# Sums and turnings of the first projection between later token spans, input rows asked for first, and modulation stores on other queues

## The reference, cut to what matters

```
for l in range(2):
    sh1, s1, g1, sh2, s2, g2 = split(silu(c) @ ada_w[l] + ada_b[l], 6)   # one set for latent, one for context tokens
    a = rmsnorm(h, norm_mix[l]) * (1 + s1) + sh1
    y = mixer_ab(a) if l == 0 else mixer_c(a)      # gated DeltaNet + short conv | windowed attention with sinks
    h = h + g1 * y
    f = rmsnorm(h, norm_ffn[l]) * (1 + s2) + sh2
    h = h + g2 * hier_moe(f)                       # top-2 of 32 experts
return rmsnorm(h_latent, norm_final)

def mixer_ab(a):                                   # its first step is the projection that this case is about
    z = a @ w_in                                   # columns: q, k, v, gate, two rates per head, b, c, h
    q, k, v = split(silu(conv3(z[qkv])), 3)
    q, k = l2norm(q), l2norm(k)                    # sums of squares over the 128 channels of a head
    ...                                            # delta rule over chunks, gated by silu(gate)
    y_short = b * conv3(c * h)
```

## Time and profile before

| | |
|---|---|
| median of 3 runs | 3735.29 us (3731.69 to 3741.27) |
| the profiled execution | 3731.38 us, its span 3729.6 us |
| TensorE busy | 3034.7 us, 81% of the span |
| VectorE, ScalarE, GpSimd busy | 1220.7, 677.5 and 330.9 us |
| mean granted TensorE clock | 0.922 of full speed |
| `project0`, its seven parts (L510) | 1344 matmuls, 496.5 us busy |

### The profile page before, as it was taken

One profiled execution on the slowest core, in us unless ns is written; L12 is line 12 of the kernel. 1 busy time (PEld: TensorE's weight loads), 2 busy tenths in 40 slices (PEclk: granted clock), 3 DMA queues, 4 the chain that ended last, 5 costly groups with the idle time before them and its releaser, 6 DMA issues. The chain is left out here.

```text
span 3729.6 us, 50996 instructions
## 1 busy us (share of the span) xinstructions
PE 3034.7 (81%) x18238; PEld 1579.8 (42%) x18239; DVE 1220.7 (33%) x2215; ACT 677.5 (18%) x1522; POOL 330.9 (9%) x366
## 2 busy tenths in 40 slices
PE   3899999799976957999998729958889579789991
PEld 1454455588862433333333214445554323223330
DVE  3313313467664342111111061246653511001114
ACT  2212112111121110000000031146661100000002
POOL 0000000121210000000000032211110000000002
PEclk9999999899997977999999959979999689999995
DMA  6411110223234436778988351131101379886874
GB/s 268 149 49 51 35 44 28 80 77 97 70 142 172 175 159 262 292 302 337 395 312 325 145 210 39 40 126 52 42 22 47 153 293 398 332 370 252 359 298 163
DMA packets 152814, 667.46 MB, mean 179 GB/s; under 512 B 26128, under 2 KB 62128, under 8 KB 121936
## 3 DMA queue, kind: packets, MB, share of 16 engines
q1 hardware_dynamic: 123568, 540.05, 37.8%
q0 software_dynamic: 19504, 72.03, 5.2%
q10 hardware_dynamic: 9584, 53.19, 3.4%
HBM read 595.84 MB, written 69.39 MB: 178 GB/s over the span
## 5 line engine op out<-in xcount | busy, mean ns | idle before, releaser
L1808 PE MATMUL bank<-w,xT 128*64 x3392 | 752.7, 602 | 67.2 <-DMA w<-in_moe_w 41.1
L510 PE MATMUL bank<-aT,w 128*128 128x512 f32 (+1 forms) x1344 | 496.5, 532 | 6.7 <-DVE short L692 5.9
L1808 PEld LDWEIGHTS bank<-w,xT 128*64 128x64 f32 x3392 | 254.1, 139 | 529.5 <-issue 529.3
L1828 PE MATMUL bank<-w,hT 128*64 (+1 forms) x1696 | 380.3, 601 | 55.3 <-issue 49.0
L510 PEld LDWEIGHTS bank<-aT,w 128*128 128x128 f32 x1344 | 263.6, 197 | 234.8 <-issue 219.8
L1900 DVE TENSOR_TENSOR h<-h,bank 128x512 f32<-128x512 f32 x53 | 36.5, 688 | 787.1 <-PE bank L1808 787.1
L1828 PEld LDWEIGHTS bank<-w,hT 128*64 128x64 f32 x1696 | 121.9, 138 | 277.3 <-issue 277.3
L2108 PE MATMUL bank<-at_w_in,aT 128*128 128x512 f32 x416 | 182.3, 598 | 2.9 <-PEq L116 2.9
L2299 PE MATMUL bank<-eye,probs 128*128 128x128 f32 x640 | 99.0, 286 | 45.2 <-ACT probsT L2363 45.0
L1757 POOL DMA_INDIRECT x<-moe_x,idx_block x55 | 53.3, 970 | 841.4 <-PE bank L1784 839.7
L2108 PEld LDWEIGHTS bank<-at_w_in,aT 128*128 128x128 f32 x416 | 79.1, 192 | 99.8 <-issue 99.8
(11 more groups left out here) (339 smaller groups left out, 3924.7 us busy)
## 6 DMA issues: line engine op xcount, KB each, us to landing
w<-in_moe_w SPq DMA_DIRECT2D x180, 2048.0 KB, 8.9
ada_w<-in_ada_w SPq DMA_DIRECT2D x48, 1024.0 KB, 7.9
moe_y<-y ACTq DMA_DIRECT2D x53, 512.0 KB, 10.4
w<-in_moe_w ACTq DMA_DIRECT2D x12, 2048.0 KB, 31.5
w<-in_ab_w_in SPq DMA_DIRECT2D x28, 512.0 KB, 3.8
moe_y<-zero POOLq DMA_DIRECT2D x1, 8192.0 KB
moe_x<-a SPq DMA_DIRECT2D x13, 512.0 KB, 2.6
at_w_in<-in_at_w_in SPq DMA_DIRECT2D x3, 2048.0 KB
```

Of the source, the lines that this page charges most:

```text
L510: mm = pe.matmul(k.bank[3 * s + n][:, 0:width], w[j][:, c, :], aT[:, c, at:at + width], start=(c == 0), stop=(c == KC - 1))
L1808: mm = pe.matmul(k.bank[UP[half]][u * UNIT:(u + 1) * UNIT, :], xT[:, c, u * UNIT:(u + 1) * UNIT], w13[:, r if u else ds(buf[0], 1), half, ...
L1828: mm = pe.matmul(k.bank[Y[half]][u * UNIT:(u + 1) * UNIT, :], hT[:, c, u * UNIT:(u + 1) * UNIT], w2[:, r if u else ds(buf[0], 1), at:at + ...
```

## The change

1. `begin`: SP asks for the context rows and two halves of the latent rows, each on its own semaphore, ahead of the table pieces; `eye` and `tri` come behind them. Each sum of squares waits only for its own rows. SP stores the modulation rows. POOL has nothing to do.
2. `norm_mod` and `gate_heads`: SP instead of ACT stores the modulation rows. `project_norm`: POOL stores them.
3. `project0`: a part is now made of single spans (`span`), and `turns` of single groups. The sums of k stand after two spans of part 3, the turnings of k in two pieces between the spans of part 4, those of v between the spans of part 5. ACT's square roots become `roots`, put after its next copy; ACT takes part 4 into a new tile `c_raw` before the turnings of v.
4. `combine`, layer 0: ACT takes the sum of squares of tile n-3 right after it scales tile n.
5. `attend`: `v_win` gets a semaphore of its own, which only the output products wait for.

```diff
 begin, SP
+        sp.dma_start(k.H[:, 0:CT, :], dr["ctx"].rearrange("b (t p) d -> p (b t) d", p=P)).then_inc(h_in[0], 16)
+        for n in range(2):
+            half = slice(n * LT // 2, (n + 1) * LT // 2)
+            sp.dma_start(k.H[:, CT + n * LT // 2:CT + (n + 1) * LT // 2, :], x[:, half, :]).then_inc(h_in[1 + n], 16)
         mod.loads(sp)
+        sp.dma_start(k.eye[:], dr["const_eye"]).then_inc(consts_in, 16)
+        sp.dma_start(k.tri[:], dr["const_tri"].rearrange("d p n -> p d n")).then_inc(consts_in, 16)
+        mod.store(sp)
+        sp.wait_ge(consts_in, 32)
 begin, ACT and DVE
-        act.wait_ge(h_in, 64)
         for n, t in enumerate(ours):
+            act.wait_ge(h_in[(t + 2) // 4], 16)
...
-        mod.store(act)
 norm_mod and gate_heads (project_norm likewise, on POOL)
+            mod.store(sp)
...
-            mod.store(act)
 project0, TensorE
+        def span(h, j, n):
+            s, (at, width) = j % 2, SPANS[n]
+            if n == 0:
+                pe.wait_ge(w_in[j], primed((h + 1) * 16))
+                pe.wait_ge(z_copied[s], primed(h * COPIED[s] + use(j)))
+                pe.wait_ge(z_gated[s], primed(h))
+            for c in range(KC):
+                mm = pe.matmul(k.bank[3 * s + n][:, 0:width], w[j][:, c, :], aT[:, c, at:at + width],
+                               start=(c == 0), stop=(c == KC - 1))
+            if n == 2:
+                mm.then_inc(z_ready[s], 1)
...
             part(h, 2)
+            span(h, 3, 0)
+            span(h, 3, 1)
             norms(h, 1)
-            part(h, 3)
-            turns(h, 0)
-            part(h, 4)
-            turns(h, 1)
-            part(h, 5)
+            span(h, 3, 2)
+            span(h, 4, 0)
+            span(h, 4, 1)
+            turns(h, 0, 0)
+            turns(h, 0, 1)
+            span(h, 4, 2)
+            turns(h, 0, 2)
+            span(h, 5, 0)
+            turns(h, 1, 0)
+            turns(h, 1, 1)
+            span(h, 5, 1)
+            turns(h, 1, 2)
+            span(h, 5, 2)
             part(h, 6)
 project0, ACT
             square(h, 0)
+            roots(h, 0)
...
             square(h, 1)
             raw(h, 2, x)
+            roots(h, 1)
...
             silu(h, 2)
+            act.wait_ge(z_gated[1], primed(h))
+            raw(h, 4, c_raw)
             take_turns(h, 1)
-            raw(h, 4, z)
 combine, ACT
+            if not final and n >= 3:
+                square(n - 3)
 attend
-            sp.dma_start(vw[u][:], ...).then_inc(blk_in[u], 16)
+            sp.dma_start(vw[u][:], ...).then_inc(vw_in[u], 16)
...
+            if kv == 0:
+                pe.wait_ge(vw_in[u], primed(g // KVS // 2 * 16 + 16))
```

More of the change, by code:

```diff
@@ L246, in begin @@
     c = k.sb("c", [P, 2, KC])
-    c_in, c_silu, h_in = k.sem("c_in", 0), k.sem("c_silu", 0), k.sem("h_in", 0)
+    c_in, c_silu, h_in = k.sem("c_in", 0), k.sem("c_silu", 0), [k.sem(f"h_in{n}", 0) for n in range(3)]
+    consts_in = k.sem("eye_tri_in", 0)
     mod = Modulation(k, [(0, 0)], KC, 0)
@@ L258, in _ @@
         sp.dma_start(c[:, 1, :], dr["c"].rearrange("a (p j) -> (a p) j", p=P)).then_inc(c_in, 16)
-        mod.loads(sp)
[L261 to L267, removed]
+        sp.dma_start(k.H[:, 0:CT, :], dr["ctx"].rearrange("b (t p) d -> p (b t) d", p=P)).then_inc(h_in[0], 16)
+        x = dr["x"].rearrange("b (t p) d -> p (b t) d", p=P)
+        for n in range(2):
+            half = slice(n * LT // 2, (n + 1) * LT // 2)
+            sp.dma_start(k.H[:, CT + n * LT // 2:CT + (n + 1) * LT // 2, :], x[:, half, :]).then_inc(h_in[1 + n], 16)
+        mod.loads(sp)
+        sp.dma_start(k.eye[:], dr["const_eye"]).then_inc(consts_in, 16)
+        sp.dma_start(k.tri[:], dr["const_tri"].rearrange("d p n -> p d n")).then_inc(consts_in, 16)
+        mod.store(sp)
+        sp.wait_ge(consts_in, 32)
     @block.tensor
@@ L285, in _ @@
         nc.scalar.activation(rstd[:], rstd[:], ACT.Sqrt).then_inc(root_ready, 1)
-        mod.store(act)
     @block.vector
     def _(dve):
-        dve.wait_ge(h_in, 64)
         for n, t in enumerate(theirs):
+            dve.wait_ge(h_in[(t + 2) // 4], 16)
             if n:
@@ L349, in _ @@
                     nc.scalar.copy(aT[:, 4 * half:4 * half + 4, at:at + P], src).then_inc(aT_ready, 1)
-        if mod:
-            mod.store(act)
     @block.vector
@@ L401, in project0 @@
     y = k.sb("y", [P, PADTOK])
+    c_raw = k.sb("c_raw", [P, PADTOK])
     z = k.sb("z", [P, PADTOK])
@@ L501, in _ @@
         pe.wait_ge(ab_read, primed(1))
-        def part(h, j):
[L504 to L512, removed]
+        def span(h, j, n):
[9 more added lines that the diff above has]
+                mm.then_inc(z_ready[s], 1)
+        def part(h, j):
+            for n in range(3):
+                span(h, j, n)
         def aux(h, m):
@@ L526, in norms, with turns @@
                           start=True, stop=True).then_inc(norm_ready, 1)
-        def turns(h, n):
+        def turns(h, n, g):
             if n == 0:
@@ L533, in turns @@
                 pe.wait_ge(silu_ready, primed(h * 3 + 3))
[L534 to L540, removed]
+            to = aux(h, 6 + 3 * n + g)
+            for q in range(min(4, NT - 4 * g)):
+                t = 4 * g + q
+                at = t * P + (2 if t >= CT else 0)
+                mm = pe.transpose(to[:, q * P:(q + 1) * P], z[:, at:at + P], k.eye[:])
+            mm.then_inc(norm_ready, 1)
         with pe.Fori(0, NH) as h:
@@ L590, in square, with roots @@
             nc.scalar.activation(y[:, 0:PADTOK - 2], z[:, 0:PADTOK - 2], ACT.Square).then_inc(sq_ready, 1)
+        def roots(h, n):
             for s, (_, width) in enumerate(SPANS):
@@ L682, in _ @@
                 at += 3 if n else 1
-                c = nc.vector.tensor_tensor(x[:, at:at + width], z[:, at:at + width],
+                c = nc.vector.tensor_tensor(x[:, at:at + width], c_raw[:, at:at + width],
                                             k.bank[3 + n][:, 0:width], ALU.mult)
@@ L1316, in _ @@
             sp.wait_ge(a_stored[u], primed(16 * ((T + 1 - u) // 2)))
+    if mod:
+        @block.gpsimd
+        def _(pool):
+            mod.store(pool)
     @block.tensor
@@ L1970, in root, with square @@
             nc.scalar.activation(r[:, n:n + 1], r[:, n:n + 1], ACT.Sqrt).then_inc(root_ready, 1)
+        def square(n):
+            act.wait_ge(added[n % 2], primed(n // 2 + 1))
+            if n:
+                act.wait_ge(sum_ready, primed(n))
+            nc.scalar.activation(sq[:, 0, :], H[:, first + n, :], ACT.Square, accum_out=r[:, n:n + 1]).then_inc(sum_ready, 1)
         for n in range(T):
@@ L1983, in _ @@
         else:
[L1984 to L1988, removed]
+            for n in range(T - 3, T):
+                square(n)
             act.wait_ge(mean_ready, primed(1))
@@ L2218, in attend @@
     ctx_in, vc_in, blk_in = k.sem("ctx_in"), k.sem("vc_in"), [k.sem(f"blk_in{u}") for u in R2]
+    vw_in = [k.sem(f"vw_in{u}") for u in R2]
     ctx0_ready = k.sem("ctx0_ready")
@@ L2256, in load @@
             sp.dma_start(band[u][:], dr["const_band"][b]).then_inc(blk_in[u], 16)
-            sp.dma_start(vw[u][:], dr["att_v"][b:b + 3].rearrange("t p n -> p t n")).then_inc(blk_in[u], 16)
+            sp.dma_start(vw[u][:], dr["att_v"][b:b + 3].rearrange("t p n -> p t n")).then_inc(vw_in[u], 16)
         sp.dma_start(sink[:], dr["at_sink"].to_broadcast([P, ATT_H])).then_inc(ctx_in, 16)
@@ L2281, in scores @@
             if c == 0:
-                pe.wait_ge(blk_in[u], primed(block // 2 * 64 + 64))
+                pe.wait_ge(blk_in[u], primed(block // 2 * 48 + 48))
             rows = [slice(HD * h, HD * h + HD) for h in R2]
@@ L2393, in maxima @@
             if m % PAIRS == 0:
-                dve.wait_ge(blk_in[u], primed(block // 2 * 64 + 64))
+                dve.wait_ge(blk_in[u], primed(block // 2 * 48 + 48))
             dve.wait_ge(s_ready, primed(m + 1))
```

## The result

The changed kernel took 3670.2 us (median of 4, 3666.97 to 3672.49), the kernel before 3733.49 us (median of 4, 3730.24 to 3741.27). The ratio is 0.9827, with a 95% interval of 0.9813 to 0.9841: 63 us or 1.7% faster. Forecast were 3679 us and 56.7 us less, with a range of 3664 to 3702. The profiled execution took 3672.49 us, its span is 3670.8 us.

What follows compares the result with a forecast made beforehand. TensorE, 81% busy, was taken as the bound, with waits in the first projection and slow clock behind them. Terms -44.6 - 7.9 + 0.8 - 4.6 + 0.6 - 1.0 = -56.7 us gave 3679 us, range 3664 to 3702.

Steps and rivals of the forecast that it cites:

- The covers: First projection: TensorE's other work before each moved sum or turning outlasts what it waits for, by 1.6 to 5.7 us.
- The thin one: First projection: span 0 of part 5 hides SiLU of v before v's turnings, with 1.6 us to spare.
- The size of the order's gain: First projection: each head 11.2 us shorter than 143.12 us, 44.6 us for four heads.
- part 0 behind it 19.13 (slow clock, as now): First projection: after the remaining 1.98 us wait at a head's start, part 0 still takes 19.13 us.
- The first stage: `begin`: with rows ahead of the table, the next stage starts at 48.6 us, 7.9 us less.
- their 0.4 each: `norm_mod` and `gate_heads`: four store issues on SP instead of ACT cost 0.4 us more each, 0.8 in all.
- project_norm: End of `project_norm`: POOL's early stores remove ACT's issue time and part of the landing, 4.6 us less.
- combine: `combine`: nothing gained; ACT waits for POOL's add before tile 1's square, and the last add comes 0.6 us later.
- attend: `attend`: TensorE's first scores no longer wait for `v_win`, 1.0 us less, once.
- The new wait in each head (1): First projection: ACT's chain before v's turnings is late in each head; price 16 us, time 3695; chance 0.16.
- the order buys little (2): First projection: half the waits return elsewhere, 22 of 44.6 us gained; `begin` gains nothing; 3709 us; chance 0.08.
- The clock (3): First projection: granted clock falls to 1.2 GHz behind each turning and sum, making it slower, up to 151 us; chance 0.05.

Runs made afterwards that it cites:

- The repeat: The changed kernel timed and profiled once more, nothing altered, against the kernel before: 3663.86 us against 3733.55, ratio 0.9812.
- rest_only: Kernel before with only the earlier squares in `combine` and the own semaphore for `v_win`: 3734.11 us against 3735.98, ratio 0.9994.
- order_only: Kernel before with only the first projection's new order, ACT's later roots and `c_raw`: 3681.73 us against 3735.98, ratio 0.9863.

## Why the prediction was right

The direction, the place and the mechanism held, step by step. The total was under-estimated by 7 us of 63.

- *The covers.* These carried the argument, and the profile of the changed kernel lets each be read. The rows behind them, on ACT, then DVE:

```profile
290.13 1.27 ACT L605 ACTIVATE y<-z 128x1282 f32<-128x1282 f32 x1
...
324.74 1.27 ACT L601 ACTIVATE z<-y 128x1282 f32<-128x1282 f32 x1
...
330.18 1.07 ACT L618 COPY by_token<-bank 128x512 f32<-128x512 f32 x2 [2.94 <-POOLq L483]
...
311.22 0.69 DVE L682 SCALAR_TENSOR_TENSOR z<-z,inv_norm 128x512 f32<-128x512 f32 x1
```

  The squares of k end at 291.4, the sums start at 296.97: 5.6 us (5.7 foretold). k is normalised at 311.9, its turnings start at 316.31: 4.4 (4.4). SiLU of v ends at 326.0, the turnings start at 327.72: 1.7 (1.6). ACT's first copy of v ends at about 330.7 after its wait for POOL's store, the last group starts at 335.46: about 4.7 (5). The thin one held; taking it away cost what it should.
- *The size of the order's gain.* 11.2 us per head were forecast, 14.1 came in the head shown. The largest term of the 2.9 between them is "part 0 behind it 19.13 (slow clock, as now)": in two of the three heads behind that wait the clock was full, and parts 0 and 1 took 34.45 us from start to start, not 36.13. The repeat had it slow in the second head and fast in the two behind it, so it changes between executions (the last section has the count). The rest, about 1.25 us in every head, is in terms taken a little long: turnings 2.2 us with nothing lost at the changes between kinds of work, where 2.60 + 0.5 stood, and parts of 17.2 instead of 17.27 to 17.35. The whole stage gave 52.3 us where 44.6 were forecast; of these 7.7, the two rows at full clock are 3.4, and that was luck as far as the prediction goes.
- *The first stage.* 7.9 forecast, 9.1 in the profile (8.9 in whole time when alone). The last piece of the table landed at 38.4 as worked out (38.3); TensorE's last products ran at full clock, 1.04 us instead of 1.89, and SP's four issues took 1.18, not half a microsecond more than ACT's 1.16. Nor did `norm_mod` and `gate_heads` lose their 0.4 each: over all profiles they take 44.1 and 67.0 us in the mean with ACT's stores, 43.7 and 66.8 with SP's.
- *`project_norm`.* 4.6 forecast, 4.1 in the profile and 5.8 in the mean over all profiles. POOL issued its twelve stores within 6.1 us, long before the stage's end at 1308.67:

```profile
1285.40 6.08 POOL L239 DMA_DIRECT2D mods<-rows  x12 [190.96 <-DVE rows L228]
```

- *`combine`.* 0.6 lost forecast, 0.2 in the profile. The wait that was foretold is there, beside the earlier trace rows:

```profile
2107.79 4.82 POOL L1987 TENSOR_TENSOR H<-H,y 128x1024 f32<-128x1024 f32 x2
2110.33 1.06 ACT L1999 ACTIVATE squares<-H 128x1024 f32<-128x1024 f32 x1 [8.30 <-POOL H L1987]
...
2133.94 1.06 ACT L1999 ACTIVATE squares<-H 128x1024 f32<-128x1024 f32 x1 [3.72 <-POOL H L1987]
```

  ACT waits 8.30 us, POOL's first two adds take 4.82 us instead of 5.80, and the last square, counted from the first gather, begins 0.2 us later.
- *`attend`.* Here the step failed in full, if by 1 us: the first scores start 10.4 us after the stage's first DMA instead of 11.2, and the stage is as long as before. The term priced the first wait only and put the new semaphore at nothing. Each block's first output products now have a wait more in front of them. The second block, before and changed:

```profile
2520.51 0.65 PE L2309 MATMUL bank<-diag,ones 128*64 128x256 f32 x4
2521.07 1.51 PE L2321 MATMUL bank<-probsT,v_win 128*64 128x256 f32 x12
```

```profile
2460.74 0.65 PE L2338 MATMUL bank<-diag,ones 128*64 128x256 f32 x4
2461.41 1.52 PE L2352 MATMUL bank<-probsT,v_win 128*64 128x256 f32 x12
```

  From start to start it is 0.67 us instead of 0.56, and the profile lists no wait for `v_win` there. The first block's products are 0.76 us early, counted from the stage's first DMA, and each block behind it gives back about 0.11, until the eighth is 0.04 late. `rest_only` shows the same steps; `order_only`, without this edit, shows none.
- *The rivals.* The new wait in each head (1) did not come. That the order buys little (2) is out: 54 us came from it alone. Of (2) the half about the transfers was right as a danger: on two queues rows and table do share them, and the single queue avoids it. The clock (3) did not fall behind turnings. The Trainium skill (TensorE: Matmul & The Clock Gate, Part 4: PE-mode transpose) says that a transpose does not count as busy TensorE in the same way. Groups of 0.2 to 0.9 us between spans, at clock 1.00, show no harm from it here; runs of more than ten turnings were not tried.

## What to carry to other kernels

A wait of the busiest engine is best removed by moving its dependent step to where the longest chain behind it is surely done, and the cover can be computed beforehand from the old trace to a few tenths of a microsecond; but move the whole chain, since a step put later makes its followers late (the turnings left in place cost the stage 37 to 40 us). Where a stage ends in a chain that needs the last bytes of one transfer, ask for everything else ahead of it in the same queue, and let the side work start on its own semaphore. A semaphore added for the sake of one early wait is paid at each of its waits, 0.11 us here. When single stages are compared between two profiles, look first how far the unchanged ones differ: here 10 us in one of them.

## What was not expected of the hardware

The same wait was followed by different clocks. After 1.98 us without work at a head's start, parts 0 and 1 took 36.30 us (clock 0.91 in the first of them) or 34.61 us (1.00). In the four kernels with the old order, each of the twelve such rows has 36.30. In the seven profiles with the new order or most of it, the wait is the same to the hundredth, and 8 of 21 rows have 36.30, in different heads in two executions of one kernel. So the slow clock there was rarer with the new order. Why is open. It is not only what TensorE does in the 37 us before, since the kernel with the turnings back ends its heads as the old order does, with the same rows, and has 36.30 once in three. The old heads all had nearly one length (143.1 to 143.5 us), the others 129 to 141; no run tests whether that matters.

The first head varies too, with either order. Its parts 0 and 1 stand behind small products and a wait of 0.80 us, and took 34.61 us in six of the twelve profiles and 36.30 to 37.62 in the other six. In two profiles of one kernel this was the largest part of the difference between their stages.

After 1.64 us no slow stretch showed in any of the four heads; after 4.83 us and more the sums behind the wait took twice their time in every head (4.40 us at clock 0.50 in the earlier trace rows). A short wait costs its own length, and sometimes nearly as much again (1.98 us, then 1.69).
